# Where the steps of an adaLN weight stand in a two-block transformer kernel: opening, router, layer seam, and two copies

## The chip, the cores and the metric

One core of a Trainium2 chip. The metric is the device time of one execution in microseconds (us), as the median of several runs. The engines of the core are TensorE (PE, matmuls and transposes), VectorE (DVE), ScalarE (ACT), GpSimd (POOL) and SyncE (SP, which here issues the weight loads). Each runs its own instruction stream in order; they meet at semaphores.

## What is computed

Two blocks of two layers each, over one sequence of 256 rows and a width of 1024, in float32. The part that the change is about is the modulation of the first block: `mod` comes from a vector `c` and one 1024 x 6144 matrix per layer, w_ada.

```python
def first_block(x, c, w_ada, b_ada, w_in, ...):
    cond = jax.nn.silu(c)
    for l in range(DEPTH):                                  # 2
        mod = cond @ w_ada[l] + b_ada[l]
        sh1, sc1, g1, sh2, sc2, g2 = [m[:, None, :] for m in jnp.split(mod, 6, axis=-1)]
        h = _layer_norm(x) * (1.0 + sc1) + sh1
        mix = _mixer(h, w_in[l], ...)       # q, k, v of two attentions, gates, w_pa, w_pb, w_out
        x = _layer_norm(DN_ALPHA * x + g1 * mix, ln1_g[l], ln1_b[l])
        h = _layer_norm(x) * (1.0 + sc2) + sh2
        ffn = _moe(h, w_router, ...)        # 16 experts, 2 for each row, from the best of 4 groups
        x = _layer_norm(DN_ALPHA * x + g2 * ffn, ln2_g[l], ln2_b[l])
    return x

def hybrid_layer(x, mem, ...):              # second block, twice
    h = rms_norm(x, norm_mix_g)
    rq, rk, rv, rg, pv, nq, nk, nv, mq = jnp.split(h @ w_in, 9, axis=-1)
    # retention, pooling, neighbourhood attention, memory attention; each gated and projected
    # x += merged @ w_out;  x += ffn(rms_norm(x))  with a hidden width of 2816
```

## The kernel before

**Weights.** All large weights come in 310 units of 1 MB (128 partitions x 2048 float32). For each, SP loads `raw` (L468), ACT copies it to `whi`, rounded to fp32r (`hi`, L1326), DVE makes the rest, `low = raw - whi` (`lo`, L1916), and PE multiplies in three products: `mm3`, L546 (hi x hi), L547 (lo x hi), L548 (hi x lo). There are 6 `raw` and 4 `whi` buffers in a ring, so SP runs ahead by a few units. The rows that are multiplied are split in the same way: `lift` transposes 128 of the 256 rows on PE into two PSUM banks (L564; t = 0 and t = 1 are the two halves of the rows), DVE and ACT scale and shift one bank each (DVE L1964, ACT L1369), ACT rounds them to `Hh` (L1376), and DVE makes `Hl` (L1969).

**w_ada.** The two matrices are cut in 48 steps of 1 MB, numbered 0 to 47, 24 for each layer. A step (`mod_step`, L644) is 4 matmuls of 32 x 512 in float32 (8 in the profile) out of one 1 MB buffer. Two steps fill one row of sums, which ACT copies out of PSUM (`mod_out`, L1411); `mod_sums(j)` (L663, 4 matmuls of 128 x 1) turns that row into columns, and DVE adds the bias (`mod_fin`, L1933). Part j needs steps 2j and 2j+1 (for the first four: 0 and 2, 1 and 3, and so on). Where each step and each sum stands among PE's other work is said by two tables of named places, `MOD_TAKEN` and `MOD_SUMMED` (L218 to L221), read by `mod_turn` (L650, L1413, L1935) on PE, ACT and DVE; `mod_slot` says in which buffer a step is loaded (`ada`, `TB`, pieces of `G` and `AR`), so that a later step with the same buffer loads only after the earlier one was taken. Layer 1 (l=0) needs parts 0 to 11, layer 2 parts 12 to 23. Steps 0 to 7 and their sums stand ahead of everything else (L1300 and on).

**Order.** Nothing is scheduled by a planner: `program_pe`, `program_act`, `program_dve`, `program_pool` and `program_sp` each write out their engine's order. The places that the change touches, in the order of time: the opening; `moe` of l=0 with the new x transposed for the router (xT, L940), the logits (L950, L956), place `rt` (L956 and on), the place matmuls (L967), the gather of the rows in the order of their experts (L979), the expert loop over n (`gate_up`, `down`); the seam, that is the end of `moe(0)` with three steps behind `put_back`, then layer 2's lift; the projections and attention of layer 2 with places qa, vd1, vd2, qk0 to qk5, at0 to at9; and in the second block the projections (`second_block` on ACT, where rq, rk and others are squared, L1741, and their transposes copied, L1382) and `out_proj` (L621), whose four units make 2 x 2 banks and which has the first half's transposes of the following lift (`turn_first`) ahead of its third unit for the second half of the rows.

**PSUM.** The 8 banks are handed out in a fixed rotation: `bank` (L308) takes the one that was left longest ago and waits until those who read it are done, `leave` (L316) gives it back. So who takes a bank first decides for whom it waits. In `first_block` both banks of qa are taken ahead of the first product:

```python
                b = [bank(pe, "qa", l, t) for t in range(2)]
                bk, bv = bank(pe, "ka", l), bank(pe, "vd", l, 0)
                for t in range(2):
                    for a in range(2):
                        H_ready(sid, t, a)
                        part(us[a], a, t, b[t]).then_inc(*up("mm", "qa", l, t, a))
```

## Time and profile before

| | us |
|---|---|
| median of 3 runs | 1797.58 (1797.54 to 1797.79) |
| the profiled execution | 1800.65 |
| its span | 1798.8 |
| PE busy in it | 1709.0 (95%) |
| DVE busy | 1171.6 (65%) |
| ACT busy | 939.8 (52%) |
| mean granted PE clock | 0.976 |

The span runs from the first to the last instruction of the profiled execution. All times of the timeline are counted from its start. A timeline row is a run of like instructions: start, time that they cover, engine, line, operation, what it writes and reads, how many, and in brackets how long the engine sat idle before it and what it waited for. A row of a group of stretches gives, for each stretch, each engine's busy time and number of instructions, then the clock that PE was granted as a share of full speed, the busy share of the DMA engines, and GB/s.

### The profile page before, as it was taken

To read this page: it belongs to the slowest core of one execution; us is meant where nothing else is said; L and a number is where in the kernel's file an instruction comes from. 1 tells how busy PE (TensorE), PEld (TensorE's weight loads), DVE (VectorE), ACT (ScalarE), POOL (GpSimd) and SP (SyncE) were. 2 spreads that over 40 slices of the span, in tenths; PEclk is the share of its full clock that TensorE was granted. 3 is DMA by queue.
4 is the path that set the end of the run, shared out by engine and by line. 5 is a ranking of instruction groups with operands and counts; after the bars stand their busy time and mean duration, and the time that the engine had idled before them with its cause. 6 is when DMAs were issued, how large, how long until landed. Compare 5 with 4: busy or idle time off the path is not lost.

```text
span 1798.8 us, 27507 instructions
## 1 busy us (share of the span) xinstructions
PE 1709.0 (95%) x11564; PEld 1506.1 (84%) x11564; DVE 1171.6 (65%) x1288; ACT 939.8 (52%) x1057; POOL 224.6 (12%) x209
## 2 busy tenths in 40 slices
PE   4999997999889999799989999999999999999999
PEld 2888885888678888588869889899999989989998
DVE  2537658899864766889987475565446756665443
ACT  4435535877543554678756454354445545354442
POOL 0330010000024001001004400200001610210000
PEclk9999998999989999899989999999999999999999
DMA  9985566999848525499956445466655644546552
GB/s 363 320 275 181 176 212 235 363 373 374 289 146 282 175 101 190 181 382 376 358 178 222 120 138 165 141 211 211 207 184 184 188 130 129 188 141 209 186 186 76
DMA packets 207306, 393.28 MB, mean 219 GB/s; under 512 B 6129, under 2 KB 143345, under 8 KB 191313
## 3 DMA queue, kind: packets, MB, share of 16 engines
q1 hardware_dynamic: 204768, 381.71, 61.3%
q0 software_dynamic: 1712, 7.50, 1.2%
q10 hardware_dynamic: 704, 2.33, 0.4%
q8 instruction: 92, 1.51, 0.3%
q14 instruction: 30, 0.24, 0.0%
HBM read 390.46 MB, written 1.05 MB: 218 GB/s over the span
## 4 chain that ended last, share of the span: by engine, by line
PE 74%; DVE 9%; ACT 5%; POOL 5%; issue 5%; DMA 1%; SPq 0%; POOLq 0%; DVEq 0%; ACTq 0%
PE ps L546 21%; PE ps L548 21%; PE ps L547 21%; DVE low L1916 3%; PE ps L644 2%; ACT whi L1326 2%; POOL TB L2799 1%; PE ps L847 1%; PE ps L815 1%; DMA AR<-in_w_ada 1%; PE ps L830 1%; PE ps L663 1%; PE ps L564 1%; DVE small L1978 1%; POOL T L2692 1%
## 5 line engine op out<-in xcount | busy, mean ns | idle before, releaser
L1916 DVE TENSOR_TENSOR low<-raw,whi 128x2048 fp32r<-128x2048 f32 x310 | 714.6, 2315 | 393.5 <-ACT whi L1326 391.8
L1326 ACT ACTIVATE whi<-raw 128x2048 fp32r<-128x2048 f32 x310 | 591.4, 1913 | 335.3 <-PE ps L548 305.5
L546 PE MATMUL ps<-Hh,whi 128*128 128x256 f32 x1536 | 438.8, 286 | 0.0
L547 PE MATMUL ps<-Hl,whi 128*128 128x256 f32 x1536 | 434.4, 283 | 0.0
L548 PE MATMUL ps<-Hh,low 128*128 128x256 f32 x1536 | 434.4, 283 | 0.0
L546 PE MATMUL ps<-whi,Hh 128*128 128x256 f32 (+1 forms) x896 | 294.4, 329 | 27.1 <-DVE T L1964 9.9
L546 PEld LDWEIGHTS ps<-Hh,whi 128*128 128x128 f32 x1536 | 294.3, 192 | 17.4 <-issue 16.9
L547 PEld LDWEIGHTS ps<-Hl,whi 128*128 128x128 f32 x1536 | 294.4, 192 | 0.5
L548 PEld LDWEIGHTS ps<-Hh,low 128*128 128x128 f32 x1536 | 294.4, 192 | 0.0
L547 PE MATMUL ps<-low,Hh 128*128 128x256 f32 (+1 forms) x896 | 289.7, 323 | 0.0
L548 PE MATMUL ps<-whi,Hl 128*128 128x256 f32 (+1 forms) x896 | 289.4, 323 | 0.0
L546 PEld LDWEIGHTS ps<-whi,Hh 128*128 128x128 f32 x896 | 174.7, 195 | 49.1 <-DVE T L1964 9.9
L548 PEld LDWEIGHTS ps<-whi,Hl 128*128 128x128 f32 x896 | 174.4, 195 | 12.5
L547 PEld LDWEIGHTS ps<-low,Hh 128*128 128x128 f32 x896 | 174.7, 195 | 11.5
L546 PE MATMUL ps<-whi,Bh 128*128 128x512 f32 x336 | 134.6, 401 | 0.2
L547 PE MATMUL ps<-low,Bh 128*128 128x512 f32 x336 | 131.3, 391 | 0.0
L548 PE MATMUL ps<-whi,Bl 128*128 128x512 f32 x336 | 131.2, 391 | 0.0
L548 PE MATMUL ps<-whi,Gr 128*128 128x512 f32 x192 | 74.8, 390 | 0.0
L546 PE MATMUL ps<-whi,Gr 128*128 128x512 f32 x192 | 74.7, 389 | 0.0
L547 PE MATMUL ps<-low,Gr 128*128 128x512 f32 x192 | 74.7, 389 | 0.0
L2667 POOL TENSOR_SCALAR small<-small 128x1 f32<-128x1 f32 (+2 forms) x30 | 15.7, 524 | 470.8 <-ACT AR L1723 184.2
L548 PEld LDWEIGHTS ps<-whi,Bl 128*128 128x128 f32 x336 | 63.1, 188 | 13.5
(325 smaller groups left out, 2161.5 us busy)
## 6 DMA issues: line engine op xcount, KB each, us to landing
raw<-in_w_gu SPq DMA_DIRECT2D x80, 1024.0 KB, 5.6
raw<-in_w_ff SPq DMA_DIRECT2D x66, 1024.0 KB, 5.1
raw<-in_w_in SPq DMA_DIRECT2D x58, 1024.0 KB, 5.9
raw<-in_w_d SPq DMA_DIRECT2D x40, 1024.0 KB, 5.7
raw<-in_w_gate SPq DMA_DIRECT2D x32, 1024.0 KB, 5.4
ada<-in_w_ada SPq DMA_DIRECT2D x18, 1024.0 KB, 7.1
G<-in_w_ada SPq DMA_DIRECT2D x16, 1024.0 KB, 8.4
raw<-in_w_out SPq DMA_DIRECT2D x16, 1024.0 KB, 5.0
```

Of the source, the lines that this page charges most:

```text
L546: pe.matmul(out, lhs[0], rhs[0], start=start, stop=False)
L547: pe.matmul(out, lhs[0], rhs[1], start=False, stop=False)
L548: return pe.matmul(out, lhs[1], rhs[0], start=False, stop=stop)
L564: ins = pe.transpose(b[:, j * P:(j + 1) * P], src[:, t, k * P:(k + 1) * P], ident)
L644: ins = pe.matmul(b[32 * k:32 * k + 32, :], cpad[:, 4 * a + k, :], mod_slot[s][:, 512 * k:512 * k + 512], start=a == 0, stop=a == 1)
L663: ins = pe.matmul(b[:, i:i + 1], acc[:, i * P:(i + 1) * P], ones[:, 0:1], start=True, stop=True)
L815: ins = pe.matmul(b[:, qt * S:(qt + 1) * S], q[o:o + 64], k[o:o + 64], start=True, stop=True)
L830: ins = pe.transpose(b[:, kt * S + qt * P:kt * S + (qt + 1) * P], Sb[:, qt, g * S + kt * P:g * S + (kt + 1) * P], ident)
L847: ins = pe.matmul(b[64 * half:64 * half + 64, 0:S], v, pair_turned(p, g, half)[:, kt * S:(kt + 1) * S], start=g + kt == 0, stop=(g, kt) == ...
L1326: act.activation(wide(i, whi), wide(i, raw), ACT.Copy).then_inc(*up("w_hi", i))
L1916: dve.tensor_tensor(wide(i, low), wide(i, raw), wide(i, whi).bitcast(F32), ALU.subtract).then_inc(*up("w_lo", i))
L1978: step(dve.tensor_reduce(mx, src, AX.X, ALU.max))
```

## The change

1. **Opening.** PE: the transposes of half 0 only, then steps 4 to 7 and the sums of 2 and 3, then the transposes of half 1 (before: both halves, then the steps). The second qa bank is taken when half 1 begins. ACT: copies of rows 2 and 3, hi(0), lift of half 0, hi(1) to hi(3), the load of the table `rows` (656 KB; before it was issued ahead of the copies of rows 2 and 3), lift of half 1. DVE: lo(0) stands between the scaling of half 0 and its `Hl`; lo(1) to lo(3) ahead of the lift of half 1.
2. **Router and seam.** A new place `x1` behind xT's half 0 takes steps 31 to 33 (31 was at rt; 32 and 33 at the seam). rt takes the sums of part 15 (before in the expert loop) and steps 34 and 35; the expert loop at n = 2 the sums of 16 and 17 (before of 15); the seam steps 36 to 41 and the sums of 18 (before steps 32 to 34). Layer 2 keeps steps 42 to 47, at vd2, qk1, qk2, qk4, at0, at1, and five sums, 19 to 23, at vd1, vd2, qk2, qk5, at2 (before: 13 steps and 8 sums). Steps 32, 33 and 35 are loaded into two new buffers over `Bh` and `Bl`; loads 32 and on are issued at other points of SP's program.
3. **Second block, ACT.** The copy of rqT stands one place sooner, before the square of nk, that of rkT before the hi of the unit behind nv.
4. **Second block, `out_proj`.** `turn_first` comes ahead of the fourth unit instead of the third.

```diff
+MOD_TAKEN = [{"qa": (8, 9)} | {place: (10 + i,) for i, place in enumerate(MOD_PLACES[1:22])}
+             | {"x1": (31, 32, 33), "rt": (34, 35), "ff": (36, 37, 38, 39, 40, 41)},
+             {"vd2": (42,), "qk1": (43,), "qk2": (44,), "qk4": (45,), "at0": (46,), "at1": (47,)}]
...
         def mod_acc(j):
-            return AR[:, 8448:8960] if j in (1, 3) else AR[:, 7936:8448]
+            return AR[:, 8448:8960] if j in (1, 3, 16, 18, 20) else AR[:, 7936:8448]
...
@@ program_sp
-            for s in (29, 30):
+            load_mod(sp, 29)
+
+            sp.wait_ge(*at("mm", "pv", 0, 2, 2))
+            load_mod(sp, 30)
+            load_mod(sp, 31)
+            load(number["A", 0, "pa", 1] + 7)
+
+            sp.wait_ge(*at("mm", "pa", 0, 3))
+            load_mod(sp, 32)
+            load_mod(sp, 33)
+            load(number["A", 0, "out", 3] + 7)
+            for s in (34, 35, 36):
                 load_mod(sp, s)
-            load(number["A", 0, "out", 3] + 7)
-            for s in (31, 32):
-                load_mod(sp, s)
 
             sp.wait_ge(*at("mm", "gather", 0, 3))
-            for s in (33, 34):
+            for s in (37, 38):
                 load_mod(sp, s)
             load(number["A", 1, "qa", 0] + 6)
-            for s in (35, 36):
+
+            sp.wait_ge(*at("y_lo", 0, 0, 1))
+            sp.wait_ge(*at("y_lo", 0, 1, 1))
+            for s in (39, 40, 41, 42):
                 load_mod(sp, s)
...
@@ out_proj
-                    if turn_first and i == 2:
+                    if turn_first and i == 3:
                         turn_first()
@@ first_block, PE
-                b = [bank(pe, "qa", l, t) for t in range(2)]
+                b = bank(pe, "qa", l, 0)
                 bk, bv = bank(pe, "ka", l), bank(pe, "vd", l, 0)
                 for t in range(2):
+                    if t:
+                        b = bank(pe, "qa", l, 1)
...
@@ moe, PE
+                    if t == 0:
+                        mod_turn(l, "x1")
...
                 if l == 0:
-                    for s in (32, 33, 34):
+                    for s in MOD_TAKEN[0]["ff"]:
                         mod_step(s)
+                    mod_sums(18)
@@ program_pe
-            for t in range(2):
-                lift(("A", 0, 1), xn, t, "a_norm", "A", 0, 1, t)
+            lift(("A", 0, 1), xn, 0, "a_norm", "A", 0, 1, 0)
             for s in range(4, 8):
                 mod_step(s)
             mod_sums(2)
             mod_sums(3)
+            lift(("A", 0, 1), xn, 1, "a_norm", "A", 0, 1, 1)
@@ moe, ACT
                 mod_turn(l, "xT")
+                mod_turn(l, "x1")
                 taken("A", l, "out", 3)
                 x_turned(1)
@@ first_block, ACT
                 if l == 0:
-                    mod_out(2)
-                    mod_out(3)
                     hi(0)
-                    hi(1)
                     lift(sid, modc(0, 1), modc(0, 0), 0, ("mod_cols", 3))
-                    hi(2)
+                    for i in range(1, 4):
+                        hi(i)
+                    act.dma_start(rows[:, :], dr["rows"].partition_broadcast(P)).then_inc(*up("rows_in", by=16))
                     lift(sid, modc(0, 1), modc(0, 0), 1)
-                    hi(3)
                 else:
                     taken("A", 0, "d", NT - 1)
+                    for j in (18, 19):
+                        mod_out(j)
                     ln(sid, 0)
-                    mod_out(16)
+                    mod_out(20)
@@ second_block, ACT
                 taken("B", l, "nq")
+                leave_bank(tile["rqT"], ("T", "rq", l), "T_a", "rq", l)
                 square("nk", l, (("mm", "nk", l), ps("nk", l)), ("head_d", "nq", l))
                 taken("B", l, "nk")
-                leave_bank(tile["rqT"], ("T", "rq", l), "T_a", "rq", l)
+                leave_bank(tile["rkT"], ("T", "rk", l), "T_a", "rk", l)
                 taken("B", l, "nv")
-                leave_bank(tile["rkT"], ("T", "rk", l), "T_a", "rk", l)
@@ residual_and_lift, DVE
                 lift(sid, scale, bias, 0, *ready)
+                mod_turn(0, "ff")
                 half(1, 1)
@@ first_block, DVE
-                    lo(0)
-                    lift(sid, modc(0, 1), modc(0, 0), 0, "mod_cols", 3)
-                    lo(1)
+                    lift(sid, modc(0, 1), modc(0, 0), 0, "mod_cols", 3, between=lambda: lo(0))
+                    for i in range(1, 4):
+                        lo(i)
                     lift(sid, modc(0, 1), modc(0, 0), 1, "mod_cols", 3)
-                    lo(2)
-                    lo(3)
```

The line numbers of the changed kernel are 18 to 26 higher at the same instructions: a step is L664 there, sums are L683, the lift's transposes L584, the products L566 to L568.

PE's order at the opening, before, from the lift's first transposes (`cons_s,T1`) over the steps (`cpad`) and sums (`ones,AR`) to the first product; psN is the PSUM bank:

```order
L564 MATMUL ps4<-cons_s,T1 128x128 x4
L564 MATMUL ps5<-cons_s,T1 128x128 x4
L564 MATMUL ps6<-cons_s,T1 128x128 x4
L564 MATMUL ps7<-cons_s,T1 128x128 x4
L644 MATMUL ps0<-AR,cpad 32x512 x4
L644 MATMUL ps1<-AR,cpad 32x512 x4
L644 MATMUL ps0<-T2,cpad 32x512 x4
L644 MATMUL ps1<-ada,cpad 32x512 x4
L663 MATMUL ps2<-ones,AR 128x1 x4
L663 MATMUL ps3<-ones,AR 128x1 x4
L546 MATMUL ps4<-whi0,Hh 128x512
```

And PE's order at the same place with the change:

```order
L584 MATMUL ps4<-cons_s,T1 128x128 x4
L584 MATMUL ps5<-cons_s,T1 128x128 x4
L664 MATMUL ps6<-AR,cpad 32x512 x4
L664 MATMUL ps7<-AR,cpad 32x512 x4
L664 MATMUL ps6<-T2,cpad 32x512 x4
L664 MATMUL ps7<-ada,cpad 32x512 x4
L683 MATMUL ps0<-ones,AR 128x1 x4
L683 MATMUL ps1<-ones,AR 128x1 x4
L584 MATMUL ps2<-cons_s,T1 128x128 x4
L584 MATMUL ps3<-cons_s,T1 128x128 x4
L566 MATMUL ps4<-whi0,Hh 128x512
```

The second pair of transposes moved from ahead of the four steps to behind the sums, and into other banks; the first product takes the same bank, ps4, that half 0's transposes were in.

PE's order at the router of l=0, before: `cons_s,xs` are xT's transposes, `T,wpad` and `cons_s,AR` the logits, `TB,ones` the place matmuls, `ada,cpad` steps:

```order
1233 L644 MATMUL ps<-ada,cpad 32x512 x4
1234 L940 MATMUL ps<-cons_s,xs 128x128 x16
1235 L950 MATMUL ps<-T,wpad 32x256 x8
1236 L956 MATMUL ps<-cons_s,AR 128x16 x2
1237 L644 MATMUL ps<-ada,cpad 32x512 x4
1238 L967 MATMUL ps<-TB,ones 128x12 x2
```

And PE's order there with the change (`Bf` are the new buffers):

```order
1234 L664 MATMUL ps<-AR,cpad 32x512 x4
1235 L962 MATMUL ps<-cons_s,xs 128x128 x8
1236 L664 MATMUL ps<-ada,cpad 32x512 x4
1237 L664 MATMUL ps<-Bf_55,cpad 32x512 x4
1238 L664 MATMUL ps<-Bf_56,cpad 32x512 x4
1239 L962 MATMUL ps<-cons_s,xs 128x128 x8
1240 L974 MATMUL ps<-T,wpad 32x256 x8
1241 L980 MATMUL ps<-cons_s,AR 128x16 x2
1242 L683 MATMUL ps<-ones,AR 128x1 x4
1243 L664 MATMUL ps<-ada,cpad 32x512 x4
1244 L664 MATMUL ps<-Bf_55,cpad 32x512 x4
1245 L991 MATMUL ps<-TB,ones 128x12 x2
```

Three steps now stand between the two halves' transposes, and one set of sums and two steps, where one step stood, ahead of the place matmuls.

PE's order at the seam, before: `Gr,ARr` is `put_back`'s last multiplication, `cons_s,T` the transposes of layer 2's lift, half 0:

```order
1995 L1052 MATMUL ps<-Gr,ARr 128x512 x8
1996 L644 MATMUL ps<-ada,cpad 32x512 x4
1997 L644 MATMUL ps<-AR,cpad 32x512 x8
1998 L564 MATMUL ps<-cons_s,T 128x128 x8
1999 L546 MATMUL ps<-whi,Hh 128x512
```

And PE's order there with the change:

```order
2002 L1076 MATMUL ps<-Gr,ARr 128x512 x8
2003 L664 MATMUL ps<-ada,cpad 32x512 x4
2004 L664 MATMUL ps<-AR,cpad 32x512 x12
2005 L664 MATMUL ps<-ada,cpad 32x512 x4
2006 L664 MATMUL ps<-AR,cpad 32x512 x4
2007 L683 MATMUL ps<-ones,AR 128x1 x4
2008 L584 MATMUL ps<-cons_s,T 128x128 x8
2009 L566 MATMUL ps<-whi,Hh 128x512
```

Six steps and one set of sums stand where three steps stood.

## Rows read from the trace of the kernel before

**Rows 1.** The page's part 1: busy time, share and instructions.

```profile
PE 1709.0 (95%) x11564; PEld 1506.1 (84%) x11564; DVE 1171.6 (65%) x1288; ACT 939.8 (52%) x1057; POOL 224.6 (12%) x209
```

**Rows 2.** PE's waits by line: waited for: us in total, times, longest us.

```profile
PE ps L1137 <- ACT AR L1382: 3.1, 2, 1.6
```

**Rows 3.** Timeline of PE, opening.

```profile
20.35 3.57 PE L663 MATMUL ps<-ones,AR 128*128 128x1 f32 x16
...
28.13 3.64 PE L644 MATMUL ps<-AR,cpad 128*32 128x512 f32 x16
...
33.61 1.92 PE L663 MATMUL ps<-ones,AR 128*128 128x1 f32 x16
45.41 0.77 PE L546 MATMUL ps<-whi,Hh 128*128 128x512 f32 x1 [9.88 <-DVE T L1964]
```

**Rows 4.** Timeline of ACT, opening.

```profile
33.73 0.60 ACT L1411 ACTIVATE AR<-ps 128x512 f32<-128x512 f32 x1 [0.26 <-PE ps L644]
```

**Rows 5.** Timeline of DVE, opening.

```profile
36.16 2.29 DVE L1916 TENSOR_TENSOR low<-raw,whi 128x2048 fp32r<-128x2048 f32 x1 [0.43 <-ACT whi L1326]
...
40.42 1.29 DVE L1969 TENSOR_TENSOR Hl<-T,Hh 128x512 fp32r<-128x512 f32 x2 [0.69 <-ACT Hh L1376]
...
43.84 1.36 DVE L1964 TENSOR_SCALAR T<-ps,modT 128x128 f32<-128x128 f32 x4
```

**Rows 6.** Loads: SP's timeline, step 7's landing, GB/s in 12:45 (40 slices).

```profile
14.77 2.58 SPq L438 DMA_DIRECT2D ada<-in_w_ada  x1
...
DMA to landing us min/median/max: 14.7/14.7/14.7
...
GB/s 377 395 390 387 377 392 392 385 380 392 392 377 387 390 392 377 390 390 390 377 432 409 385 405 375 392 390 386 361 353 344 351 348 349 345 363 384 390 390 377
```

**Rows 7.** Timeline of PE, router of l=0.

```profile
279.56 1.06 PE L940 MATMUL ps<-cons_s,xs 128*128 128x128 f32 x8 [3.02 <-DVE xs L2013]
...
285.33 1.94 PE L644 MATMUL ps<-ada,cpad 128*32 128x512 f32 x8
288.35 1.00 PE L967 MATMUL ps<-TB,ones 128*128 128x12 f32 x4 [1.08 <-DVE TB L2096]
```

**Rows 8.** Busy time by stretch: router (two), seam, layer 2's projections.

```profile
281.00:295.00 14.00, 10.26 (x53) 7.18 (x54) 10.77 (x38) 3.90 (x7) 0.55 (x1) 0.51 0.23 77
295.00:308.00 13.00, 8.52 (x47) 6.78 (x45) 11.81 (x20) 9.27 (x12) 1.10 (x2) 1.00 0.79 292
...
493.00:506.00 13.00, 6.00 (x18) 4.79 (x19) 9.54 (x19) 4.26 (x8) 2.07 (x2) 0.50 0.06 23
...
526.00:560.00 34.00, 34.00 (x281) 29.50 (x280) 19.55 (x16) 15.23 (x17) 29.06 (x30) 1.00 0.90 299
```

**Rows 9.** Timeline of PE, seam.

```profile
485.58 1.06 PE L644 MATMUL ps<-ada,cpad 128*32 128x512 f32 x8
486.47 1.90 PE L644 MATMUL ps<-AR,cpad 128*32 128x512 f32 x16
495.64 1.94 PE L564 MATMUL ps<-cons_s,T 128*128 128x128 f32 x8 [7.28 <-ACT T L1346]
```

**Rows 10.** Seam's last load: SP's timeline; DMA issues (KB, us to landing).

```profile
487.57 0.37 SPq L438 DMA_DIRECT2D AR<-in_w_ada  x1
...
AR<-in_w_ada SPq DMA_DIRECT2D x1, 1024.0 KB, 7.0
```

**Rows 11.** Timeline of ACT, second block's projections, first layer.

```profile
1002.05 1.92 ACT L1326 ACTIVATE whi<-raw 128x2048 fp32r<-128x2048 f32 x1
1003.85 0.60 ACT L1382 ACTIVATE AR<-ps 128x512 f32<-128x512 f32 x1
```

**Rows 12.** Timelines of PE and DVE, second block's out, first layer.

```profile
1170.59 1.03 PE L564 MATMUL ps<-cons_s,T 128*128 128x128 f32 x8
...
1173.36 1.12 DVE L1962 TENSOR_SCALAR T<-ps,cols_s 128x128 f32<-128x128 f32 x4
...
1187.42 1.06 PE L564 MATMUL ps<-cons_s,T 128*128 128x128 f32 x8 [1.54 <-ACT T L1353]
```

50 lines of the change are left out of this document (26 added, 24 removed).

## The prediction

> **What bounds the kernel now.** I read the page first: TensorE (PE) is busy 95% of the span [rows 1]. So a matmul that goes from a stretch in which PE never stops shortens the kernel by its full length, one that moves into a wait of PE costs nothing, and outside that only PE's waits can be won. Then the waits by line: the second block has two of 1.6 us for a copy of ScalarE (ACT) [rows 2]. Last the timelines around each place that the diff touches, where a row's brackets tell how long the engine sat idle and for whom: 9.88 in the opening for VectorE (DVE) [rows 3], 3.02 in the router [rows 7], 7.28 at the seam between the layers [rows 9]. The forecast is a sum over six places.
>
> Durations: the profiled execution took 1800.65 us with a span of 1798.8, 0.17% above the median 1797.58. I sum in the profile's microseconds and take the sum off the median, since a scaling by 0.17% moves it by 0.02.
>
> **1. The opening.** Now PE transposes both halves for the lift, then takes steps 4 to 7 of w_ada from 28.13, then the sums of 2 and 3, and waits 9.88 us until 45.41 for DVE's lift of half 1 [rows 3]. That wait is for a PSUM bank: the first products take both qa banks at once, and the second is one that half 1's transposes hold until DVE's L1964, from 43.84 for 1.36, has read it. What the first products need of data, DVE had finished long before: H_lo of half 0 was made from 40.42 on, 0.65 for its first half [rows 5]. The change takes qa's second bank later, so this wait goes; and it puts half 1's transposes behind the steps, so the chain before DVE's lift of half 0 is shorter. Worked forward: steps 4 to 7 start at 25.75, right behind half 0's transposes. Their loads were issued in the order of their numbers, the last, step 7's, at 14.8, and it landed 14.7 later, at 29.5 [rows 6], so they don't hold them up. At half clock a step takes 1.8 (3.64 for two), so 4 to 6 end near 31.0 and step 7 near 32.3 (before 33.65). ACT's copy of its row (0.60, before at 33.73 [rows 4]) then ends at 33.0, the sums at 33.95, DVE's columns of part 3 at 34.3. DVE: lift 1.36, to 35.7; lo(0), put between, 2.29 [rows 5], to 38.0; H_lo's first half 0.65, to 38.65. ACT meanwhile makes hi(0), 1.9, to 34.9, and its share of the lift, no longer than DVE's by more than a few tenths, to about 36.4, then H_hi, while DVE is at lo(0) to 38.0; so ACT isn't last. First product at 38.8 instead of 45.41: **-6.6**. Behind it PE wants lo(1) after 5.2 us of products at half clock (44.0; DVE has it at 42.5 or before) and half 1 after ka's first half, past 50; DVE reaches that at about 49. The bounds: -8 if the clock is up sooner, so that the steps end by 31, and -5 if lo(1) to lo(3) or the loads behind the w_in units come in too late once.
>
> The load of `rows` (656 KB), moved behind hi(3) on ACT, gave its place to raw 0 to 3. At 390 GB/s [rows 6] it is worth 1.7 us to them. The Trainium skill, "DMA: Bandwidth & Descriptors", section "Issuing engines are not separate DMA queues", says that transfers issued by different engines share the same hardware engines and interleave; by that rule the gain is real. Without it raw 0 would land as late as before and the opening would gain up to 0.7 less.
>
> **2. The router of layer 1 (l=0).** Steps 31, 32, 33 go behind the transposes of half 0, where PE waits 3.02 us [rows 7]; three steps at full clock are 3 x 0.89 = 2.7 (start to start [rows 9]), so they fit, and cost nothing if their loads are there; SyncE issues them after the products of pv and pa, well before out's own. At rt, before the place matmuls, there were 1.94 of step 31 and 1.08 of wait [rows 7], at half clock (0.51 from 281 to 295 [rows 8]). Now there are one set of sums, 1.78 at half clock (3.57 for two [rows 3]) and two steps, 3.88. That is 3.7 more, of which the wait takes 1.08: +2.6. ACT has two more copies of 0.6 ahead of its second transposed half, which is on the way to the logits (PE waits for it): +0.7. The gather behind is 32 matmuls at half clock, and with PE fed for longer part of it may run at full clock; half a microsecond comes back, an estimate: the 10.26 us of PE's work from 281 to 295 at 0.51 [rows 8] hold some 5 that half clock adds, and I give a tenth of them. **+2.8**, bounds 0 (clock up over the whole stretch: everything takes half and fits in the waits) and +3.3. In the expert loop one set of sums more, where PE is the bound: **+0.9**.
>
> **3. The seam.** Now 3 steps (ada, 2 x AR) from 485.58 on, then 7.28 us of wait, then half 0's transposes at 495.64 [rows 9]. The change puts six steps and a set of sums there. What the first ones take is hidden in those 7.28 us. What counts is the last: step 41 needs its buffer after step 37, and its load is third, behind 39 and 40. Before, the second of two such loads, issued at 487.57, landed 7.0 later, at 494.6 [rows 10], and 1 MB takes 2.7 at 390 GB/s [rows 6]. Load 39 waits only for y's low halves, some 1.5 us before the old first could go: then 41 lands at 494.6 + 2.7 - 1.6 = 495.7. If 39 starts no sooner, at 497.3; if 40 and 41 keep the old times, at 494.6. Step 41 at half clock (0.50 from 493 to 506 [rows 8]) takes 1.94, and the sums behind it 1.78: transposes at 499.4 instead of 495.64. I take a little less, since one part of this may still run at full clock. Everything behind (DVE's lift, H_lo, DVE's L1997 whose bank the first product waits for) moves along with it, as DVE does these in the order of the program: **+3.5**, bounds +2 and +4.5.
>
> One figure of the Trainium skill bears on this. The same page, section "Where 436 GB/s comes from", puts transfers from HBM at about 358 GB/s for a core, 2.93 us for 1 MB. By it three loads in a row take 0.7 longer, the seam's term would be +4.2 and the total 0.7 higher. The row of 390 GB/s speaks against it, and I keep to the row.
>
> **4. Layer 2.** There 13 steps and 8 sums stood, and 6 and 5 stay. From 526 to 560 PE is busy 34.00 of 34.00 us [rows 8], so each is paid in full: 7 x 0.89 + 3 x 0.9 = 8.9. One sum stood in a stretch that DVE sets, and its going wins little there: 0.9 less. **-8.0**, bounds -7 and -9. This is the term that I trust most: the work isn't gone, but it is moved to places where PE waited (1, 2, 3) and its price there is in those terms.
>
> **5. Second block, copies.** Twice PE waits 1.6 for ACT's copy of rkT [rows 2]. That copy (0.60 at 1003.85) stands behind a whi of 1.92 started at 1002.05 [rows 11]. With the copy ahead of it, it is done 1.9 sooner, more than the wait. What is late next: rqT, moved ahead of a square in the same way; it came at 1001.6 and comes sooner. The square waits 0.6 more and its head sums follow 0.6 later, off PE's path. **-3.0**, bounds -3.2 and -1.5 (if the whi pushed back by 0.6 is wanted at once).
>
> **6. Second block, out.** Half 0's transposes come one part (12 matmuls of 512 columns, 2.7 us) later. Before they ran at 1170.59, but DVE took its share of the lift only at 1173.36, behind a low [rows 12]. Now they end at about 1174.3, and DVE's share starts at 1174.4: 1.0 later, not 2.7. What follows on DVE and ACT in their order (H_hi, H_lo, the next units' halves, the sum of half 1's rows, its norm) moves with it, and at its end PE waits already, 1.54 before half 1's transposes at 1187.42 [rows 12]. So that wait grows by 0.95, at two places: **+1.9**, bounds 0 (the lift isn't on that path) and +2.2.
>
> The sum: -6.6 + 2.8 + 0.9 + 3.5 - 8.0 - 3.0 + 1.9 = **-8.5**. Median 1797.58 - 8.5 = 1789.1, so 1789.0; the profile's span 1790.3.
>
> **The rivals.**
> (a) *The filler fits.* PE's clock stays up over the router since PE is fed there, all of the moved steps vanish in the waits (router 0.2, seam +2). For it: the clock was low from 281 on, behind the wait of 3.02, which is now filled. Against it: the waits on the way to the logits stay. Sum -12.6: 1785.0.
> (b) *The opening gives half.* PE starts at 38.8 but then waits for lo(1), H_lo of half 1 or the units behind, which DVE has no earlier than before. For it: DVE made four low's, both lifts and H_lo until 51, and still must. Against it: the products before half 1 are qa's 24 matmuls and ka, some 12 us at half clock. -2.5 instead of -6.6: 1793.2.
> (c) *The late turns cost the clock.* If PE's wait at out, 1.54 now, grows to 2.5 and half clock follows it, as it does the 3.02 at the router, then the 12 matmuls behind it cost 2.7 more; at two places, less what DVE's wait hides, +3.5 over the forecast: 1792.6.
> (d) *Slower.* The router and the seam end up with more low clock, not less: PE's work from 295 to 311, now at full clock, and the first 12 us behind the seam's end, from 506, run at half clock since each stretch begins with a longer wait for DVE, whose queue has grown by mod_fin. Price: PE works 8.5 of the 13 us from 295 to 308 at clock 1.00 [rows 8], which would take twice that, and 6 us of work behind the seam likewise: +14.5, so 1803.6. It decides where 17 us more than before run at half clock: then PE loses the 8.5 that the rest gains. Against it: the clock was back at 295 after the waits of 3.02, 1.24 and 1.08 in the same stretch, and the change fills two of these.
> (e) *Not what it says*: PE waits at the seam for a load put behind others, so that the new places hold everything up, +4 to +8 there, 1793 to 1797.
>
> **How the numbers follow.** Forecast 0.60 (its own range 1785.5 to 1792.5), (a) 0.14, (b) 0.09, (c) 0.08, (d) 0.05, (e) 0.04. About 0.2%, 3.6 us, is what a measurement of this kernel tells from no change: the bounds are 1794.0 and 1801.2. Faster: the forecast, (a) and most of (b) and (c), 0.86; same: the rest of these, (e) and a fifth of (d), 0.10; slower: the rest of (d), 0.04. The range of 1784 to 1794 takes in (a), (b), (c) and the forecast's bounds nearly whole, and leaves out (d), (e) and some of the tails, 0.15 to 0.2.
>
> **What would show it.** Opening: first product at 38.8, no wait of more than 1 behind it. Router: the three steps inside the wait before the second transposes, place at 291 to 292 in the time of before. Seam: half 0's transposes 3 to 4 later against step 36 than before (10.1). Layer 2: no step between the transposes of half 1 and vd2. Second block: no wait at L1137. Wrong if the first product is past 41, if the seam's new steps wait for a load for over 3 us beyond 495.6, or if the clock stays at 0.5 past the first 14 us behind either place.

## The result and the profile after

The changed kernel takes **1783.01 us** (median of 4 runs, 1782.4 to 1783.82) against 1797.68 for the kernel before, measured beside it (1797.54 to 1798.06). The ratio is 0.9918, with a 95% interval of 0.9901 to 0.9936: 14.7 us less, with an interval of 11.5 to 17.8. Forecast were 1789.0 and a range of 1784 to 1794. So the direction was right, the gain was forecast at 8.5 and is 14.7, and the time lies 1 us below the range. A second measurement on another chip, told below, gave 0.9918 again. A granted clock of 1.00 is 2.4 GHz, one of 0.50 is 1.2.

The page's busy times and PE's waits by line, changed kernel (waited for: us in total, times, longest us):

```profile
PE 1704.7 (96%) x11564; PEld 1501.6 (84%) x11564; DVE 1172.0 (66%) x1288; ACT 939.2 (53%) x1057; POOL 222.0 (12%) x209
```

```profile
PE ps L566 <- DVE low L1942: 7.8, 9, 1.7
...
PE ps L566 <- DVE Hl L1996: 5.4, 2, 3.9
PE ps L962 <- DVE xs L2040: 5.3, 2, 5.0
```

PE does the same instructions as in [rows 1], and its longest wait behind the start is now 5.0 us. The wait of [rows 2] for the copies isn't there any more. (In such a table a wait is put down to the engine that came last by the profile.)

**Where the time went.** Both kernels make the same 9552 three-fold products in nearly the same order, so I took, for each of them, the start in the trace after less the start in the trace before. That difference stays constant where both run alike and steps where they don't:

| place | forecast | the difference in the first two traces |
|---|---|---|
| opening, to the first product | -6.6 | -8.6 |
| router of l=0, to the first expert product | +2.8 | +2.85 |
| expert loop, from n = 0 to n = 1 | none | -3.6 |
| one set of sums more in the expert loop | +0.9 | +0.9 |
| seam | +3.5 | +4.9 |
| layer 2 | -8.0 | -9.4 |
| copies, 2 places | -3.0 | -2.8 |
| later turns, 2 places | +1.9 | +1.8 |
| sum | -8.5 | **-14.0** |
| the remainder: mostly stretches of half clock elsewhere (below) | | -4.2 |

The two profiled executions, at 1800.65 and 1782.45, are 18.2 apart; the terms' own sum of 14.0 is close to the 14.7 of the medians. The third column is one pair of traces, and three of its terms move from trace to trace of the same program part: the router's between +1.2 and +3.9, the seam's between +3.9 and +4.9, and the opening's, once the clock is up on both sides, between -6.5 and -8.4. Row 15's (-3.6), the sums' and the turns' come out the same to 0.1 in each.

The opening, PE's timeline of the changed kernel, the rows that answer to [rows 3]:

```profile
23.54 1.95 PE L584 MATMUL ps<-cons_s,T 128*128 128x128 f32 x8
25.41 2.79 PE L664 MATMUL ps<-AR,cpad 128*32 128x512 f32 x16
28.04 1.03 PE L664 MATMUL ps<-T,cpad 128*32 128x512 f32 x8
29.06 1.06 PE L664 MATMUL ps<-ada,cpad 128*32 128x512 f32 x8
...
36.84 0.77 PE L566 MATMUL ps<-whi,Hh 128*128 128x512 f32 x1 [3.90 <-DVE Hl L1996]
```

The last wait of 9.88 is one of 3.90, and no longer for the lift of half 1 but for H_lo of half 0, as forecast. The steps went faster than I had them: 2.79 us for the first two instead of 3.64, and a step at full clock from 28.04 on. ACT's and DVE's timelines there, the rows that answer to [rows 4, 5]:

```profile
31.75 1.91 ACT L1351 ACTIVATE whi<-raw 128x2048 fp32r<-128x2048 f32 x1 [0.96 <-DMA raw<-in_w_in]
```

```profile
32.32 1.37 DVE L1990 TENSOR_SCALAR T<-ps,modT 128x128 f32<-128x128 f32 x4
33.69 2.29 DVE L1942 TENSOR_TENSOR low<-raw,whi 128x2048 fp32r<-128x2048 f32 x1
35.90 1.28 DVE L1996 TENSOR_TENSOR Hl<-T,Hh 128x512 fp32r<-128x512 f32 x2
```

This is the chain of the forecast, 2.0 earlier all along: lift, lo(0), H_lo, first product. hi(0) has become the row that waits for a transfer: it ends at 33.66, just as DVE gets to lo(0).

The router, PE's timeline of the changed kernel, answering to [rows 7], and the seam, answering to [rows 9]:

```profile
265.15 1.90 PE L664 MATMUL ps<-Bf,cpad 128*32 128x512 f32 x16
267.36 1.06 PE L962 MATMUL ps<-cons_s,xs 128*128 128x128 f32 x8 [0.31 <-DVE xs L2040]
270.64 1.13 PE L974 MATMUL ps<-T,wpad 128*32 128x256 f32 x16 [2.21 <-ACT T L1490]
...
272.96 1.84 PE L683 MATMUL ps<-ones,AR 128*128 128x1 f32 x8
274.73 1.93 PE L664 MATMUL ps<-ada,cpad 128*32 128x512 f32 x8
276.44 1.93 PE L664 MATMUL ps<-Bf,cpad 128*32 128x512 f32 x8
278.30 1.03 PE L991 MATMUL ps<-TB,ones 128*128 128x12 f32 x4
...
476.79 1.06 PE L664 MATMUL ps<-AR,cpad 128*32 128x512 f32 x8 [2.11 <-DMA AR<-in_w_ada]
479.58 1.93 PE L664 MATMUL ps<-ada,cpad 128*32 128x512 f32 x8 [1.72 <-DMA ada<-in_w_ada]
482.92 1.94 PE L664 MATMUL ps<-AR,cpad 128*32 128x512 f32 x8 [1.41 <-DMA AR<-in_w_ada]
...
486.52 1.95 PE L584 MATMUL ps<-cons_s,T 128*128 128x128 f32 x8
```

In the router the three steps leave 0.31 of the 3.02 us. Then the wait for ACT's transposed half is 2.21 instead of 1.24, by the two copies ahead of it (v2_seam_router below, with the copies behind, has 1.24 again), and sums and two steps, 5.3 us at half clock, fill the way to the place matmuls. At the seam each of the last three steps waits for its own load. Compared with before (13.67 earlier at this point) the transposes are 4.55 late.

### The profile page after: what moved, and what is told of

Its sections match the earlier page's. It is cut to its first block, busy times and chain, and to the rows that moved or that the text cites. A ratio compares the mean times of both kernels' runs of the same rounds, so it can differ in the third digit from the quotient of the medians.

```text
span 1780.7 us, 27507 instructions
## 1 busy us (share of the span) xinstructions
PE 1704.7 (96%) x11564; PEld 1501.6 (84%) x11564; DVE 1172.0 (66%) x1288; ACT 939.2 (53%) x1057; POOL 222.0 (12%) x209
## 4 chain that ended last, share of the span: by engine, by line
PE 77%; DVE 9%; issue 4%; ACT 4%; POOL 4%; DMA 2%; SPq 0%; POOLq 0%; DVEq 0%; ACTq 0%
PE ps L566 22%; PE ps L568 21%; PE ps L567 21%; DVE low L1942 3%; PE ps L664 2%; ACT whi L1351 2%; POOL TB L2826 1%; DMA AR<-in_w_ada 1%; PE ps L683 1%; PE ps L869 1%; PE ps L837 1%; PE ps L852 1%; PE ps L584 1%; DVE small L2005 1%; PE ps L1003 1%
## 5 line engine op out<-in xcount | busy, mean ns | idle before, releaser
L566 PE MATMUL ps<-Hh,whi 128*128 128x256 f32 x1536 | 438.6, 286 | 0.0
L568 PE MATMUL ps<-Hh,low 128*128 128x256 f32 x1536 | 434.4, 283 | 0.0
L566 PE MATMUL ps<-whi,Hh 128*128 128x256 f32 (+1 forms) x896 | 292.3, 326 | 21.3 <-DVE low L1942 7.8
L566 PEld LDWEIGHTS ps<-Hh,whi 128*128 128x128 f32 x1536 | 294.3, 192 | 15.8 <-issue 15.2
L568 PEld LDWEIGHTS ps<-Hh,low 128*128 128x128 f32 x1536 | 294.4, 192 | 0.0
L568 PE MATMUL ps<-whi,Hl 128*128 128x256 f32 (+1 forms) x896 | 287.5, 321 | 0.0
L566 PEld LDWEIGHTS ps<-whi,Hh 128*128 128x128 f32 x896 | 173.2, 193 | 42.7 <-issue 12.5
L568 PEld LDWEIGHTS ps<-whi,Hl 128*128 128x128 f32 x896 | 172.7, 193 | 12.1
L566 PE MATMUL ps<-whi,Bh 128*128 128x512 f32 x336 | 134.9, 402 | 0.2
L568 PE MATMUL ps<-whi,Bl 128*128 128x512 f32 x336 | 131.5, 391 | 0.0
L566 PE MATMUL ps<-whi,Gr 128*128 128x512 f32 x192 | 74.9, 390 | 0.1
L568 PE MATMUL ps<-whi,Gr 128*128 128x512 f32 x192 | 74.8, 390 | 0.0
L568 PEld LDWEIGHTS ps<-whi,Bl 128*128 128x128 f32 x336 | 63.2, 188 | 13.6
```

The source lines that it names most:

```text
L566: pe.matmul(out, lhs[0], rhs[0], start=start, stop=False)
L568: return pe.matmul(out, lhs[1], rhs[0], start=False, stop=stop)
```

## Experiments

Each was timed in rounds beside the kernel before on its chip. Ratios are to that kernel; 0.1% is 1.8 us.

### Opening: the bank alone, and all of it

o1_bank is the kernel before with the late qa bank:

```diff
-                b = [bank(pe, "qa", l, t) for t in range(2)]
+                b = bank(pe, "qa", l, 0)
                 bk, bv = bank(pe, "ka", l), bank(pe, "vd", l, 0)
                 for t in range(2):
+                    if t:
+                        b = bank(pe, "qa", l, 1)
                     for a in range(2):
                         H_ready(sid, t, a)
-                        part(us[a], a, t, b[t]).then_inc(*up("mm", "qa", l, t, a))
+                        part(us[a], a, t, b).then_inc(*up("mm", "qa", l, t, a))
```

> The kernel before with one edit: the second qa bank is taken only when half 1 begins. If the wait of 9.88 us in the opening was for that bank alone, the first product starts when H_lo of half 0 is there, at about 41.1 instead of 45.41, and the time falls by about 4.3 us. If the reordering of the steps around the transposes is what makes the opening of the changed kernel short, this edit alone gives under 1 us. On the clock: steps 4 to 7 still follow the 0.5 us wait between the two lifts, so they should run at half clock until about 32, as before, if that wait is what holds the clock back in the opening; if the changed kernel's earlier rise (at about 27) is only chance, it may show here too.

Measured: 1795.95, ratio 0.999 (0.998 to 0.9999). PE's timeline:

```profile
26.10 1.97 PE L564 MATMUL ps<-cons_s,T 128*128 128x128 f32 x8 [0.50 <-ACT T L1343]
28.00 2.88 PE L644 MATMUL ps<-AR,cpad 128*32 128x512 f32 x16
...
45.02 0.76 PE L546 MATMUL ps<-whi,Hh 128*128 128x512 f32 x1 [10.54 <-DVE T L1966]
```

The wait stands where it stood. My statement in the forecast, that the second qa bank is the one held, is wrong. The banks go round in a fixed order: the lift had 4, 5 (half 0) and 6, 7 (half 1); then the code takes, ahead of the first product, qa's two (4, 5) and those of **ka and vd (6, 7)**. With qa's second taken late, ka and vd get 5 and 6, and 6 is still half 1's, scaled by DVE last. The steps here also show that the clock can rise earlier in the old order: 2.88 for two steps behind the same 0.50 wait. This account of the banks is read from the code's order; a3_bank_early below tests it.

o2_opening is the kernel before with all opening edits (the diff's parts in `program_pe`, in `first_block` on PE, ACT and DVE for l=0, and the load of `rows`).

> The kernel before with all edits of the opening and none of the rest. Theory (the opening is independent of the rest): first product at 36.8 instead of 45.41, -8.5 us in the time, of which my forecast had 6.6; the 2 us beyond it come from steps 4 to 7 running at full clock from about 27 on. Rival (part of the 8.6 seen in the two profiles is only the difference of two executions, and the clock rises late in others): first product at 38 to 39, -6.6 us.

Measured: 1788.85, ratio 0.9947 (0.9933 to 0.996), so 7 to 12 us; first product at 37.01, 8.4 sooner. The first product and the time (9.5 us by the ratio) both speak for the first expectation against 6.6, and the opening doesn't need the rest of the change.

a3_bank_early is the changed kernel with the first diff above undone.

> The changed kernel with both qa banks taken ahead of the first product, as before. Late taking alone gave nothing on the kernel before. Theory now: PE waited for ka's bank, the third taken, which was half 1's first; with the transposes of half 1 moved behind the sums they lie in other banks, and nothing of the late taking is needed in the opening: no change there (first product at 36.8), within 0.3 us of the changed kernel. Rival (late taking and reordering work only together): first product past 45, +8 us or more.

Measured: 1782.51, ratio 0.9909 (0.9895 to 0.9922), against 0.9918 for the changed kernel; first product at 37.40 behind a wait of 3.80 for H_lo. So the late bank is worth nothing here: moving half 1's transposes behind the sums put them into banks 2 and 3, out of the first product's way, and that ended the wait for a bank. The rest of the gain is the shorter chain behind which the first product now waits: H_lo of half 0 came from 40.42 on before [rows 5] and from 35.90 in the changed kernel.

### Opening: the load of the table

a2_rows_early is the changed kernel with one line moved back:

```diff
             ln_act(("A", 0, 1, 1), 1, "x_in")
+            act.dma_start(rows[:, :], dr["rows"].partition_broadcast(P)).then_inc(*up("rows_in", by=16))
             mod_out(2)
...
-                    act.dma_start(rows[:, :], dr["rows"].partition_broadcast(P)).then_inc(*up("rows_in", by=16))
```

> The changed kernel with the load of the table rows issued where it was before, ahead of ACT's copies of rows 2 and 3. Theory: in the changed kernel hi(0) waits for raw 0 (0.96 us, at 31.75), so 656 KB of other load ahead of it cost their full 1.7 us at 390 GB/s: raw 0 lands at 33.4 to 33.6, the first product comes 1.7 later and the time rises by 1.7. Rival (transfers of the two issuing engines don't take from each other, or DVE's chain covers it): no change, within 0.4 us.

Measured: 1783.36, ratio 0.9922 (0.9906 to 0.9937). ACT's and PE's timelines:

```profile
33.53 1.91 ACT L1351 ACTIVATE whi<-raw 128x2048 fp32r<-128x2048 f32 x1 [2.35 <-DMA raw<-in_w_in]
```

```profile
38.62 0.77 PE L566 MATMUL ps<-whi,Hh 128*128 128x512 f32 x1 [5.30 <-DVE Hl L1996]
```

In the trace it is as the theory has it: hi(0) 1.78 later, first product 1.78 later. hi(0) starts between 31.75 and 32.11 in the eight other traces with the new opening, so its 33.53 is no scatter; the first product lies between 36.84 and 38.01 in them, so its 38.62 is less clear. The transfer issued by ACT takes its time from SP's. The time itself can't tell 1.8 us apart at this width of interval, so for the total this one stays open; the mechanism is read from the two rows.

### The wait that was named for the wrong thing

r1_row15 is the kernel before with ACT's copy of row 15 moved:

```diff
                 act.activation(R[:, 0:32], R[:, 96:128], ACT.Sigmoid).then_inc(*up("scores", l))
+                mod_turn(l, "rt")
...
-                    if n == 0:
-                        mod_turn(l, "rt")
```

> The kernel before with one edit: ACT copies row 15 (of step 31) right behind the sigmoid, at about 287.5, instead of inside the expert loop at 308.02. Theory: PE's wait of 2.76 us at 305.90 is not for DVE's low, as the row names it, but for the PSUM bank of step 31, which ACT's copy holds until 308.6; then the wait falls to 0.7, the half clock behind it (308.45 to 311.86) goes too, and the time falls by 2.1 to 3.6 us. Rival (the wait is for the low, or for the weight's load behind two w_ada loads): no change, within 0.5 us, and the wait stays at 2.8.

Measured: 1793.03, ratio 0.9974 (0.9962 to 0.9985), 4.7 us less (2.7 to 6.8). First the kernel before, PE and ACT, then r1_row15, PE and ACT:

```profile
308.66 0.80 PE L546 MATMUL ps<-whi,Hh 128*128 128x512 f32 x1 [2.76 <-DVE low L1916]
```

```profile
308.02 0.59 ACT L1411 ACTIVATE AR<-ps 128x512 f32<-128x512 f32 x1
```

```profile
306.08 0.47 PE L546 MATMUL ps<-whi,Hh 128*128 128x512 f32 x1 [0.70 <-DVE low L1915]
```

```profile
286.34 0.60 ACT L1411 ACTIVATE AR<-ps 128x512 f32<-128x512 f32 x1 [1.26 <-PE ps L644]
```

The row of before puts 2.76 us down to DVE's low. But PE starts again at 308.66, and ACT's copy ends at 308.61. In PE's instruction stream the first product of n = 1 carries two waits, and the second is the copy's:

```
L546 MATMUL ps0<-whi1,Hh 128x512 [waits c_w_lo,c_mod_row]
```

ps0 is the bank that steps 30 and 31 were summed in, from 274 on. The rotation comes back to it with n = 1, while ACT has its copy of it behind the first silu of the expert loop and a whi. Moved to where ACT is idle, it ends the wait, and the half clock that followed it (0.57 between 308 and 312) is gone too: -3.6 in the difference of the products there (-3.1 with the router ahead of it, where this trace had half clock for 3.4 us longer). The changed kernel moves this copy as a side of part 2 and gets the same 3.6. My forecast didn't have the term.

### Part 2 alone

s1_steps is the kernel before with the two tables, the places, the loads and buffers of the change, and nothing else.

> The kernel before with part 2 of the change alone: the steps and sums moved to router, expert loop and seam. By my forecast the terms are +2.8 (router) +0.9 (expert loop) +3.5 (seam) -8.0 (layer 2): -0.8 us. By the two profiles they are +2.85, then -3.6 for row 15's earlier copy, +0.9, +4.9, -9.4: -4.4 us. A time within 1 us of the kernel before's would speak for the forecast's terms, one 4 to 5 below for those read from the profiles.

Measured: 1792.89, ratio 0.9968 (0.9953 to 0.9984), 5.7 us less (2.9 to 8.4). The differences of the products: router +1.6, row 15 -3.6, sums +0.9, seam +4.0, layer 2 -9.4. The forecast's -0.8 is excluded, the -4.4 read from the traces isn't. Router and seam come out 1.3 and 0.9 lower than in the first trace of the changed kernel. The router's code is the same in both: what differs is the half clock there, 10.2 us in two pieces against 13.7.

### Copies and turns

b1_copies is the kernel before with part 3:

```diff
                 taken("B", l, "nq")
+                leave_bank(tile["rqT"], ("T", "rq", l), "T_a", "rq", l)
                 square("nk", l, (("mm", "nk", l), ps("nk", l)), ("head_d", "nq", l))
                 taken("B", l, "nk")
-                leave_bank(tile["rqT"], ("T", "rq", l), "T_a", "rq", l)
+                leave_bank(tile["rkT"], ("T", "rk", l), "T_a", "rk", l)
                 taken("B", l, "nv")
-                leave_bank(tile["rkT"], ("T", "rk", l), "T_a", "rk", l)
```

> The kernel before with part 3 of the change alone, the copies of rqT and rkT sooner. Theory: the two waits of 1.57 at L1137 are gone and the time falls by 2.8 to 3.0 us. Rival (the hi pushed back by 0.6 is missed by PE at once, or part of the 1.4 a place seen in the profiles belongs to the clock): -1.5 or less.

Measured: 1794.78, ratio 0.999 (0.9981 to 0.9999), so 0.2 to 3.4 us. The difference of the products steps by some -1.4 at each of the two places, -2.8 in all, and PE's waits by line have no row for these copies any more. The time agrees with both expectations, the trace with the first.

a1_turn_back is the changed kernel with the turns where they were:

```diff
-                    if turn_first and i == 3:
+                    if turn_first and i == 2:
```

> The changed kernel with the second block's turns put back to the third part of out. Theory: the later turns cost 0.95 us at each of two places, so the time falls by 1.9 us against the changed kernel, to about 1781.1, and in the traces the step of 0.9 at 1171 and at 1599 is gone. Rival (the cost seen there belongs to the copies moved in the same layer, which changes which unit DVE is at): no change in the time, and the 0.9 stays.

Measured: 1781.81, ratio 0.9904 (0.9888 to 0.9919) against 0.9918, whose intervals overlap; the difference of the products to the changed kernel steps by -0.88 and -0.90 at the two places (on PE's timeline of the changed kernel at 1162.21 and 1589.27). So this part of the change costs 1.8 us, the size that was forecast, but not by the wait that was named. PE's timeline of the changed kernel:

```profile
1162.21 0.39 PE L566 MATMUL ps<-whi,Hh 128*128 128x256 f32 x1 [0.73 <-DVE low L1942]
...
1169.77 1.06 PE L584 MATMUL ps<-cons_s,T 128*128 128x128 f32 x8 [1.54 <-ACT T L1378]
```

The wait before half 1's transposes is 1.54 as before and hasn't grown. The new one is 0.73 for a low, 7.6 us ahead of it, and neither the kernel before nor a1_turn_back has it: DVE takes its share of the lift later, as the forecast has it, and so makes the next low later, which PE wants at once.

### A cheaper seam, and a cheaper router

v1_seam is the changed kernel with this:

```diff
@@ moe, PE
-                    for s in MOD_TAKEN[0]["ff"]:
+                    for s in range(36, 41):
                         mod_step(s)
-                    mod_sums(18)
@@ first_block, PE
                 if l:
                     lift(sid, xn, 0, "a_norm", *sid, 0)
+                    mod_step(41)
+                    mod_sums(18)
@@ first_block, ACT
                     ln(sid, 0)
-                    mod_out(20)
                     lift(sid, modc(1, 1), modc(1, 0), 0, ("mod_cols", 15))
                     ln(sid, 1)
+                    mod_out(20)
@@ residual_and_lift, DVE
                 lift(sid, scale, bias, 0, *ready)
-                mod_turn(0, "ff")
                 half(1, 1)
+                mod_turn(0, "ff")
```

> The changed kernel, but in the seam only steps 36 to 40 stand ahead of half 0's transposes; step 41 and the sums of 18 stand behind them, in the 4.4 us for which PE waits there, and ACT's and DVE's parts of them move behind too. Theory: the seam's cost of 4.9 us is step 41's load and the half-clock step and sums ahead of the transposes; they then start at about 481.8 instead of 486.5 and the time falls by 4.2 to 4.9. Rival (the seam's cost comes from the load traffic or from ACT's copies of rows 18 and 19 ahead of the norm): under 1 us is won.

Measured: 1779.13, ratio 0.9892 (0.9876 to 0.9907). PE's timeline:

```profile
481.81 1.93 PE L664 MATMUL ps<-ada,cpad 128*32 128x512 f32 x8 [2.53 <-DMA ada<-in_w_ada]
483.67 1.97 PE L584 MATMUL ps<-cons_s,T 128*128 128x128 f32 x8
485.57 1.94 PE L664 MATMUL ps<-AR,cpad 128*32 128x512 f32 x8
...
489.73 0.47 PE L566 MATMUL ps<-whi,Hh 128*128 128x512 f32 x1 [1.07 <-DVE G L2025]
```

The transposes come right behind step 40; step 41 and the sums now lie in the wait for DVE's G, which is 1.07 instead of 4.36. In the difference of the products the seam is 5.5 cheaper, 0.6 more than its whole cost in the changed kernel; half clock lasted 10 us there and not 20. So the 4.9 was the last load, one half-clock step and the sums ahead of the transposes, and not the load traffic or ACT's copies of rows 18 and 19, which both stay. (The run also moves the copy of row 20 and DVE's part of the sums behind; what these give by themselves wasn't tested.)

v2_seam_router adds to this the turns at the third part, ACT's copies of rows 15 and 16 behind the copy of the logits, and

```diff
-             | {"x1": (31, 32, 33), "rt": (34, 35), "ff": (36, 37, 38, 39, 40, 41)},
+             | {"x1": (31, 32, 33), "rt": (34,), "gu": (35,), "ff": (36, 37, 38, 39, 40, 41)},
@@ gate_up, PE
                         spent[u[0]] = "gu", l, n, a
+                        if n == 0 and a == 0:
+                            mod_turn(l, "gu")
```

with the same place on ACT.

> The same with the turns of the second block back at the third part, ACT's copies of rows 15 and 16 put behind the copy of the logits, and step 35 taken inside the expert loop's first gate_up, where PE waits 1.7 us. Theory: -4.5 (seam) -1.9 (turns) -2.4 (router: place matmuls at 276 instead of 278.3) = -8.8 us against the changed kernel, about 1774. Rival (the router's time hangs on DVE's chain, and the half clock holds whatever is moved): the router gives under 0.5, -6.5 in all.

Measured: **1773.81**, ratio 0.9859 (0.9844 to 0.9874): 25 us below the kernel before, about 10 below the changed one. The three gains add in the difference of the products: seam -5.7, turns -1.8, router -3.2 against the first trace of the changed kernel. Against other traces with that router, which cost 1.2 to 3.9, the last would be 1.5 to 4.2. This is the best of all kernels here. Its PE timeline at the router:

```profile
273.08 1.12 PE L976 MATMUL ps<-T,wpad 128*32 128x256 f32 x16 [1.24 <-ACT T L1493]
...
277.10 1.93 PE L664 MATMUL ps<-ada,cpad 128*32 128x512 f32 x8
279.13 1.00 PE L993 MATMUL ps<-TB,ones 128*128 128x12 f32 x4
```

v3_more went one further (step 34 into the expert loop, step 40 behind the transposes, the sigmoid sooner):

```diff
-             | {"x1": (31, 32, 33), "rt": (34,), "gu": (35,), "ff": (36, 37, 38, 39, 40, 41)},
+             | {"x1": (31, 32, 33), "gu": (34,), "gv": (35,), "ff": (36, 37, 38, 39, 40, 41)},
```

> The best variant so far with three more moves: step 34 also goes into the expert loop's first gate_up (35 behind its second half), ACT's sigmoid comes ahead of its rounding of the second half's rows, and step 40 also goes behind half 0's transposes in the seam. Theory: the place matmuls come 0.6 us sooner since only DVE's chain is left ahead of them, half 0's transposes at the seam 1.8 sooner and the first product 0.9, less 0.3 for the second step in the expert loop: -1.2 us, about 1772.6. Rival (PE's new steps in half clock take all of it back at the seam, where step 40, 41 and the sums now need 5 us in a wait of 4.4): no change or +0.5.

Measured: 1781.08, ratio 0.9912 (0.9898 to 0.9926): 9.5 us worse than v2_seam_router by the ratios. Both expectations were wrong. Of it, 7.8 lie at one place in the difference of the products, in the expert loop, at 309 to 315 on its timeline. ACT's and PE's timelines:

```profile
307.42 1.91 ACT L1355 ACTIVATE whi<-raw 128x2048 fp32r<-128x2048 f32 x1 [9.46 <-DMA raw<-in_w_d]
```

```profile
312.20 0.66 PE L1052 MATMUL ps<-cons_s,T 128*128 128x128 f32 x2 [3.23 <-DVE T L2251]
315.07 0.77 PE L566 MATMUL ps<-whi,Bh 128*128 128x512 f32 x1 [2.21 <-DVE Bl L2256]
```

And SP's timeline of v3_more:

```profile
290.89 0.37 SPq L449 DMA_DIRECT2D ada<-in_w_ada  x1
291.37 2.07 SPq L449 DMA_DIRECT2D AR<-in_w_ada  x2
293.85 0.40 SPq L482 DMA_DIRECT2D raw<-in_w_d  x1
```

Load 36 goes to the buffer of step 34, and SP waits for that step; with step 34 at 290 instead of 277 this load, and 37 and 38 behind it on SP, all go out just ahead of the expert loop's next weights (in v2_seam_router load 36 was issued at 279.09 and the other two at 287.64). Three loads of 2.7 us stand in the queue: the weight issued at 293.85 lands 13.6 us later, the same one in v2_seam_router, issued at 292.14, 8.6 later, and ACT waits 9.46 for it. No run takes step 34 back by itself, so this is read from the rows. The place of a step is also the place of a later load: here two steps on, at the seam four (41 behind 37). The router gained nothing over v2_seam_router. At the seam the transposes came no sooner without step 40 ahead of them, since ACT's norm was what they waited for.

### The changed kernel again

> The changed kernel once more, on another chip. Between the two first profiles the products at the end stand 18.2 us apart, of which 5.2 lie in three places inside of full PE work where the kernel before had half clock for 3.4 us each and the changed one had none. Theory: those belong to the execution and not to the program; the program's own terms (-8.6 opening, +2.9 router, -3.6 row 15, +0.9 expert loop, +4.9 seam, -9.4 layer 2, -2.9 copies, +1.8 turns) make -14.0, and this profile will have such stretches in other places. Rival (the changed order itself keeps the clock up there): no such stretch before 300 us and a profile again some 18 below 1800.65.

Measured: 1783.77, ratio 0.9918 (0.9904 to 0.9931), the profiled execution 1784.34. Its busy time by stretch, over the place where the kernel before had half clock at 455 to 459, then the kernel before and the first trace of the changed one at the same place:

```profile
441.00:447.00 6.00, 6.00 (x31) 4.83 (x30) 5.76 (x6) 3.68 (x5) 0.00 (x0) 0.86 0.88 336
447.00:453.00 6.00, 6.00 (x25) 4.80 (x25) 4.48 (x6) 3.34 (x3) 0.00 (x0) 0.85 0.56 188
```

```profile
455.00:461.00 6.00, 6.00 (x21) 4.76 (x20) 4.60 (x6) 2.24 (x2) 0.00 (x0) 0.72 0.43 154
```

```profile
441.00:447.00 6.00, 6.00 (x32) 5.04 (x32) 5.88 (x7) 3.96 (x4) 0.00 (x0) 1.00 0.71 231
```

The same program has the stretch of half clock in one execution and not in the other, at a place where PE is never idle, and it costs 1.6. So the theory holds there. For the two stretches before 300 this trace has none either, as the rival has it, but four of the six traces of its variants have one, between 225 and 246. And b1_copies settles them: up to the second block's projections, at some 980 us, it runs the program of the kernel before, and its trace has neither of the two, nor the one at 455. First the kernel before, then b1_copies:

```profile
234.00:238.00 4.00, 4.00 (x26) 3.67 (x23) 0.32 (x3) 2.16 (x3) 0.00 (x0) 0.65 1.04 372
250.00:256.00 6.00, 6.00 (x23) 4.76 (x20) 2.51 (x4) 3.49 (x4) 2.24 (x3) 0.72 0.22 93
```

```profile
228.00:238.00 10.00, 9.78 (x80) 7.70 (x80) 4.91 (x9) 4.56 (x5) 0.39 (x1) 1.00 1.00 346
250.00:256.00 6.00, 6.00 (x28) 4.95 (x28) 3.86 (x4) 3.67 (x5) 2.91 (x4) 1.00 0.07 31
455.00:461.00 6.00, 6.00 (x29) 4.92 (x28) 5.75 (x6) 4.69 (x5) 0.00 (x0) 1.00 0.96 337
```

By 256 its products stand 3.4 us ahead of the kernel before's, by 462 4.5, with not one instruction changed. The three stretches aren't of one kind, though: the one at 233 comes behind a wait of 0.67 for a load, which b1_copies doesn't have either, and in four more traces a wait of 0.66 to 1.44 stands just ahead of a stretch between 225 and 239. In the 15 us ahead of the others (241 to 254, 443 to 459) PE is never idle.

## Why the prediction was wrong

Its structure held: all seven terms have their sign, and router, sums, copies and turns are right to 0.2 us. An eighth was missing, and the sum was short by 5.5 of 14.0, in four steps. Two of the agreements are luck. The turns cost what was forecast by another wait (a1_turn_back). And the router's +2.85 is one draw: over seven traces with the same router program it goes with the time at half clock there, from +1.2 (6.8 us of it) over +1.5 and twice +1.6 (10.2), then +2.9 and +3.0 (13.7), to +3.9 (17.1, the second trace of the changed kernel). The forecast took 13.7 us, the length in the one trace before, for a property of the program.

1. **A term that wasn't there (3.6 us).** The part on the router costs what PE gains and loses up to the place matmuls, and for ACT it counts only the two copies that were added. It doesn't ask what the copy of row 15 did where it stood. The forecast should have followed each moved instruction to the buffer that it frees: here a PSUM bank. r1_row15 shows it as a single edit. The row with 2.76 was on the timeline, with the name of another engine's product on it.
2. **Opening (2.0).** The step "at half clock a step takes 1.8" took the moment at which the clock rose in the one trace, about 32, for a property of the program. Over the traces of this study the clock rises between 27.6 and 32.1 in the old order and between 27.0 and 29.8 in the new one. The first product is at 36.8 to 38.0 in the new order, and 38.8 was just outside. In the second trace of the changed kernel it is at 37.5 and the miss 1.3, so part of the 2.0 belongs to the one pair of traces. The lower bound of -8 for "a clock that is up sooner" had the right reason and was 0.6 too small. The reason given for the 9.88 us, qa's second bank, was wrong (o1_bank, a3_bank_early): ka and vd held the first product up, not qa. It cost nothing, since the banks of half 1 moved away anyway; that was luck.
3. **Layer 2 (1.4).** I priced a step at 0.89 and a set of sums at 0.9 and gave up 0.9 for the sums in DVE's stretch. Where both stood together the difference of the products steps by 1.9, for a step alone by 0.9 to 1.2. What the 0.1 to 0.3 beyond the step's own time are wasn't tested. The stretch that I discounted does show, as a wait of 1.20 instead of 0.49:

```profile
596.08 1.08 PE L869 MATMUL ps<-AR 128*64 128x256 f32 x8 [1.20 <-DVE AR L2380]
```

4. **Seam (1.4 in the other direction).** The chain worked out was +3.8 to the transposes, at 499.4; I then took "a little less" for a clock that might be up. It was down (0.50 from 478 to 493), load 41 landed 0.8 later than the 495.7 worked out, and DVE's `mod_fin` of 0.3 stands ahead of the bank that the first product waits for. The working was better than the discount. By the figure of the Trainium skill that the prediction cites ("DMA: Bandwidth & Descriptors", section "Where 436 GB/s comes from", 358 GB/s) the term would have been +4.2, nearer to the 4.9. In this trace it isn't for that reason: load 40 landed 2.7 behind 39, as at 390 GB/s, and only 41 took 3.4. In three more traces with these loads steps 39 to 41 start 5.9 to 6.3 apart in all, divided otherwise (3.2 and 3.1 in a0_again), where 390 GB/s gives 5.4 and 358, by an estimate from that figure, 5.9. So three loads behind one another took longer here than the row of [rows 6]; why isn't shown.

The range's lower end of 1784 came from rival (a), the filler that fits. Its condition didn't come true in the first trace: the clock was as low in the router as before,

```profile
273.00:286.00 13.00, 11.80 (x56) 8.74 (x56) 8.33 (x35) 1.15 (x3) 0.00 (x0) 0.50 0.26 87
```

and still the time went past it. In other traces of the same router it came half true, with half clock for 6.8 or 10.2 us, but never for nothing. Rivals (b), (c), (d) and (e) didn't occur: no wait follows the first product, the wait before the second turns is 1.54 as before, half clock at the router lasts 13.7 us as before (17.1 at most in any trace) and at the seam 20.5 instead of 13.7, which is 7 more and not 17, and of the waits of 1.4 to 2.1 for loads at the seam all but the last are hidden.

## What to carry to other kernels

Where a moved instruction reads a PSUM bank out of a rotation, look up who takes that bank next and when: a wait that the trace puts down to the engine that was last may be a bank held by a small copy queued behind something long. A step that is moved takes its successor's load with it, so the order of the loads at the new time has to be priced like the step. Filler placed in a wait is free only while the work behind it that sets the end isn't delayed: put it behind the transposes that others wait for, in the wait that follows them, rather than ahead.

## What the runs showed of the hardware

The granted clock fell to half (1.2 of 2.4 GHz) for 3.4 us at places where PE had been busy without a pause, in some executions of the same program and not in others (at 455 us in the kernel before and not in b1_copies); each cost 1.6 us. Others of the same length came just behind a wait of 0.66 to 1.44 us that itself was there in some executions only. There were none to three such stretches in the first 500 us of the fourteen traces. At the start of the kernel the clock rose at 27.6 to 32.1 us behind the old order of the work, and at 27.0 to 29.8 behind the new one. Behind the waits in the router it stayed at half for 6.8 to 17.1 us with the same instructions. Two profiled executions can so differ by some 5 us for no reason in the program, and a forecast made from one of them inherits that.
